# Summing the squares of eleven norms: three VectorE additions and one matmul, or eight matmuls on TensorE

## The chip, the core and the metric

The kernel runs on one core of a Trainium2 chip, as a single launch. The metric is the device time of that launch in microseconds, lower is better. The core has five engines that work side by side and wait for each other by semaphores: TensorE (PE, matrix products into PSUM), VectorE (DVE), ScalarE (ACT), GpSimd (POOL) and SyncE (SP, which issues most transfers). Each engine runs its own instructions strictly in the order in which the program lists them.

## The reference

Two blocks of a model, one after the other, on 1024 tokens of 1024 features, all in float32. The first: norm, input product, sliding-window attention and a chunked mLSTM, output product, cross attention over a memory of 256 tokens, and a feed-forward block with a short convolution. The second: norm with scale and shift from a condition vector, an RWKV-7 recurrence beside a banded attention, output product. What the change touches is the norm over the features:

```python
def rmsnorm(x, g):
    xf = x.astype(jnp.float32)
    y = xf * lax.rsqrt(jnp.mean(xf * xf, axis=-1, keepdims=True) + RMS_EPS)
    return (y * g.astype(jnp.float32)).astype(x.dtype)
```

It is taken of x before the mixing (`mix`), of x before the cross attention (`x`), of the memory (`mem`), before the feed-forward block (`ffn`), at the end of the first block (`fin`) and at the start of the second (`n2`). The kernel works in two halves of 512 tokens, so there are eleven norms: mix0, mix1, mem (256 tokens), x0, x1, ffn0, ffn1, fin0, n20, fin1, n21.

## The kernel before

Activations lie transposed: features on the 128 partitions, in 8 tiles `k`, and 512 tokens of one half along the free dimension. Every weight product keeps float32 accuracy by splitting both factors into a high part in the f32r type and a low part, with three matmuls of 512 columns for each `k` (function `mm`, lines L1171 to L1173, and `mmN`, L1191 to L1193). A tile of a product is 24 such matmuls; the down product has 66. Weights come in slabs of 512 KB in four slots. ScalarE copies a slab's high part (L2239), VectorE subtracts it to get the low part (L1636); both run up to three slabs ahead. A slab of `w_ada` (condition product, L1211) isn't split.

A norm is a list of steps, made by `rms` in class `Order`:

- `rms_sq`: eight squares on ScalarE (L2297), one for each `k`.
- `rms_add`: VectorE adds the squares of the eight tiles in pairs of tiles (L1731 twice, L1734, L1736) until one tile of 512 columns is left.
- `rms_sum`: TensorE multiplies that tile with a matrix of ones, in plain float32 (L1202), which sums over the partitions. VectorE makes the mean (L1741), ScalarE the root (L2302).
- `rms_rcp`: the reciprocal on VectorE (L1748).
- `rms_out`: for each `k` the output on VectorE (L1760) and, where a product follows, ScalarE's bias (L2308, only `n2`) and high part (L2312) and VectorE's low part (L1755).

The order of all work is laid out once, as a list of steps from which each engine takes its own. `rms` yields its steps in entries, and `weave` or `partly` puts one entry of a norm behind one entry of a product (a tile, or half or a quarter of one by the job's `cut`). For fin1 and n21 a planner, `flow`, chooses what comes next by estimated times from the function `work`; these steps stand behind the tiles of products lo0, k0, r0, v0 (these are the first products of the second block: their tiles end in a shift on VectorE, L1704 to L1713). After v0 come the head norm kk0 (squares L2420, sum L1390) and the `lora` products (L1454), whose constants SyncE may fetch (L2633) only when x has been written aside (L2621) and all outputs of n21 are done, because they use x's place. n20 stands at the end of product down1, the last of the first block.

Of the kernel before, what the change touches and what calls it, by code (L numbers as in the profile page):

```python
# [11 lines left out]
MUL, ADD, SUB, MAX, MIN = ALU.mult, ALU.add, ALU.subtract, ALU.max, ALU.min  # L12
# [30 lines left out]
class Signals:  # L43
# [4 lines left out]
    def __init__(self, take):  # L48
        self.take, self.sems, self.n, self.value, self.marks, self.strict = take, {}, {}, {}, {}, False
# [6 lines left out]
    def on(self, name, *event, by=1):  # L56
        self.n[name] = self.n.get(name, 0) + by
        assert self.value.setdefault((name, *event), self.n[name]) == self.n[name], (name, event)
        return self.sem(name), by
# [5 lines left out]
    def at(self, name, *event):  # L65
        assert not self.strict or (name, *event) in self.value, (name, event)
        return self.sem(name), self.value.get((name, *event), 1)
# [92 lines left out]
class Memory:  # L160
# [38 lines left out]
    def work(self, a, n):  # L199
        return self.f32(W0 + a, n)  # L200
# [9 lines left out]
    def cs(self, name, a=0, b=None):  # L210
        o, w = CST[name]
        return self.fixed["cst"][:, o + a:o + (w if b is None else b)]
# [4 lines left out]
    def bank(self, b):  # L217
        return self.PS[:, 512 * b:512 * b + 512]

    def parts(self, a, b, n=512):  # L220

        hi, lo = ([self.f32r(o + k * n, n) for k in range(8)] for o in (a, b))
        fhi, flo = ([self.f32(o + k * n, n) for k in range(8)] for o in (a, b))
        return hi, lo, fhi, flo, self.f32(a, 8 * n)

    def slot_raw(self, i, k, n):
        return v3(self.f32(G0 + 2048 * i, k * n), k)
# [11 lines left out]

    def first(self):  # L240
        work, f32, small = self.work, self.f32, self.small
        self.xh = [[f32(X0 + 4096 * h + 512 * k, 512) for k in range(8)] for h in range(2)]
        self.xs = [[self.XT[:, k, 512 * h:512 * h + 512] for k in range(8)] for h in range(2)]
# [88 lines left out]
class Norm:  # L332


    def __init__(self, src, ready, gain, parts, free=(), T=512, bias=None, to=None, extra=()):
        self.src, self.ready, self.gain, self.hi, self.lo, self.sq = src, ready, gain, parts[0], parts[1], parts[2]
        self.to, self.squares = to or parts[3], parts[4]
        self.split, self.free, self.T, self.bias, self.extra = to is None, list(free), T, bias, list(extra)


# [157 lines left out]
def work(step):  # L498

    name, *x = step  # L500
    if name == "mm":
        return [("pe", 3 * (x[5] - x[4]) * (0.227 if x[0].N == 512 else 0.12))]
    if name == "mmN":
        return [("pe", 0.681 * len(x[1]) * (x[4] - x[3]))]
    if name == "band_s":
        wide = min(5, x[1] + 1) / 5
        return [("pe", 1.1 * wide + 0.1), ("v", 1.7 * wide + 0.1)]
    if name == "band_p":
        return [("v", 0.2 + 1.5 * min(5, x[1] + 1) / 5)]
    if name == "band_x":  # L510
        return [("a", 0.2 + 0.85 * min(5, x[1] + 1) / 5)]
    if name == "band_t":
        return [("pe", 0.1 + 0.55 * min(5, x[1] + 1) / 5), ("a", 0.2 + 0.6 * min(5, x[1] + 1) / 5)]
    if name == "band_o":
        return [("pe", 0.1 + 1.1 * min(5, x[1] + 1) / 5)]
    if name == "rms_out":
        return [("v", 1.45), ("a", 1.3)] if x[0][:3] != "fin" else [("v", 0.7)]
    if name == "ev_shift":
        return [("a", 0.6), ("v", 1.45)] + ([("a", 0.65)] if x[0].name[0] == "g" else [])
    return {  # L520
# [15 lines left out]
    }.get(name, [])  # L536


class Order:
# [83 lines left out]
    def slab(self, w, k0, kn, c0, cn, parts=True):  # L623
        self.slabs.append((w, k0, kn, c0, cn, parts))
        return len(self.slabs) - 1
# [74 lines left out]
    def rms(self, tag):  # L700
        n = self.norms[tag]
        yield [("rms_sq", tag)]
        yield [("rms_add", tag, 0)]
        yield [("rms_add", tag, 1), ("rms_add", tag, 2)]
        b, free = self.banks.take()
        self.banks.give(b, ("rms.v", "mean", tag))
        yield [("rms_sum", tag, b, free)]
        b, free = self.pairs.take()
        steps = [("rms_rcp", tag, b, free)]
        for k in range(8):  # L710
            steps.append(("rms_out", tag, k, b))
            if k % 2 and k < 7:
                yield steps
                steps = []
        self.pairs.give(b, ("rms.v", "o", tag, 7))
        return steps
# [434 lines left out]
def tensor_program(pe, w, m, S, o):  # L1151

    on, at, bank, pair, cs = S.on, S.at, m.bank, m.pair, m.cs
# [42 lines left out]
    def rms_sum(tag, b, free):  # L1196
        n = o.norms[tag]
        w.wait_ge(*at("cst", 0))
        for e in S.each(free):
            w.wait_ge(*e)  # L1200
        w.wait_ge(*at("rms.v", "add", tag, 2))
        pe.matmul(bank(b)[:, 0:n.T], cs("ones"), n.sq[0], start=True, stop=True).then_inc(*on("rms.pe", "sum", tag))  # L1202

    def ada_mm(t, b, free, q):
        view = m.slot_raw(q % NSLOT, 8, 128)
# [396 lines left out]
    def seq_out(cp, b, free):  # L1602
# [3 lines left out]
        for j in range(4):  # L1606
# [4 lines left out]
              win_t=win_t, win_o=win_o, gates_f=gates_f, gates_t=gates_t, ml_e=ml_e, ml_q=ml_q, ml_s=ml_s, ml_k=ml_k,  # L1611
# [10 lines left out]
def vector_program(v, w, m, S, o):  # L1622

    on, at, bank, pair, small = S.on, S.at, m.bank, m.pair, m.small
# [97 lines left out]
        v.scalar_tensor_tensor(out=out, in0=bank(b), scalar=m.mod[:, 16 + t:17 + t], in1=out, op0=MUL,  # L1722
                               op1=ADD).then_inc(*on("gemm.v", "ev", j.name, t))

    def rms_add(tag, i):

        n = o.norms[tag]
        part = lambda k, c: n.squares[:, k * n.T:(k + c) * n.T]
        if i < 2:
            w.wait_ge(*at("rms.a", "sq", tag, 4 * i + 3))  # L1730
            v.tensor_tensor(part(4 * i, 2), part(4 * i, 2), part(4 * i + 2, 2), ADD).then_inc(*on("rms.v", "add", tag, i))  # L1731
        else:
            w.wait_ge(*at("rms.v", "add", tag, 1))
            v.tensor_tensor(part(0, 2), part(0, 2), part(4, 2), ADD).then_inc(*on("rms.v", "add4", tag))  # L1734
            w.wait_ge(*at("rms.v", "add4", tag))
            v.tensor_tensor(part(0, 1), part(0, 1), part(1, 1), ADD).then_inc(*on("rms.v", "add", tag, 2))  # L1736

    def rms_sum(tag, b, free):
        n = o.norms[tag]
        w.wait_ge(*at("rms.pe", "sum", tag))  # L1740
        v.tensor_scalar(n.sq[0], bank(b)[:, 0:n.T], 1.0 / 1024, 1e-6, MUL, ADD).then_inc(*on("rms.v", "mean", tag))  # L1741
# [460 lines left out]
    def fin_part(h, k, mark):  # L2202
# [2 lines left out]
        v.tensor_tensor(lo[k], m.src2[h][k], hi[k].bitcast(F32), SUB).then_inc(*on("fin.v", "lo", h, k))  # L2205

    do = dict(mark=lambda name: S.mark("v", name), slab=slab, ev_gate=ev_gate, ev_add=ev_add, ev_swish=ev_swish,
              ev_conv_m=ev_conv_m, ev_conv_f=ev_conv_f, ev_up=ev_up, ev_shift=ev_shift, ev_out=ev_out, rms_add=rms_add,
              rms_sum=rms_sum, rms_rcp=rms_rcp, rms_out=rms_out, ada_end=ada_end, win_s=win_s, win_t=win_t, gates_f=gates_f,
              gates_log=gates_log, gates_scan=gates_scan, gates_max=gates_max, gates_exp=gates_exp, gates_t=gates_t,  # L2210
              ml_e=ml_e, ml_q=ml_q, ml_s=ml_s, ml_c=ml_c, ml_o=ml_o, mix_parts=mix_parts, cross_s=cross_s,
              cross_t=cross_t, cross_o=cross_o, hs_fin=hs_fin, hs_t=hs_t, hs_o=hs_o, band_s=band_s,
# [487 lines left out]


PROGRAMS = (tensor_program, vector_program, scalar_program, gpsimd_program, sync_program)


# [133 lines left out]
```

## Time and profile before

| | us |
|---|---|
| median of 3 runs | 2795.58 (2793.31 to 2796.35) |
| the profiled execution, its own time | 2795.58 |
| its span in the profile | 2793.7 |
| TensorE matmuls busy | 2533.4 (91%) |
| VectorE busy | 1438.5 (51%) |
| ScalarE busy | 937.4 (34%) |

Busy is the time in which an engine's instructions ran; a matmul's end is modelled, so a busy TensorE is not TensorE at its peak. The chain is the work that ended last, followed back from the end at each step to what released it. A row of the timeline gives start, length, engine, line, operation, what is written from what, the count merged into the row, and in brackets the engine's idle time before it with its releaser. SR names tensors of the f32r type, SB plain ones in SBUF, PS PSUM. A plain float32 matmul leaves two records, an f32r matmul one. Some matmul records are missing.

### The profile page before, as it was taken

To read this page: it belongs to the slowest core of one execution; us is meant where nothing else is said; L and a number is where in the kernel's file an instruction comes from. 1 tells how busy PE (TensorE), PEld (TensorE's weight loads), DVE (VectorE), ACT (ScalarE), POOL (GpSimd) and SP (SyncE) were. 2 spreads that over 40 slices of the span, in tenths; PEclk is the share of its full clock that TensorE was granted. 3 is DMA by queue.
4 is the path that set the end of the run, shared out by engine and by line. 5 is a ranking of instruction groups with operands and counts; after the bars stand their busy time and mean duration, and the time that the engine had idled before them with its cause. 6 is when DMAs were issued, how large, how long until landed. Compare 5 with 4: busy or idle time off the path is not lost.

```text
span 2793.7 us, 40671 instructions
## 1 busy us (share of the span) xinstructions
PE 2533.4 (91%) x17602; PEld 2046.9 (73%) x17602; DVE 1438.5 (51%) x2444; ACT 937.4 (34%) x1572; POOL 82.2 (3%) x61
## 2 busy tenths in 40 slices
PE   4997878898988999999999998988999999589879
PEld 3785656787777878888888886756777777377757
DVE  5725665537332465544555545745344454666653
ACT  3323342224332333332333324354222232233341
POOL 0000000000000000000000000002000000200000
PEclk9998986889999999999999999978999999699989
DMA  4331110444411233333333333322312320211033
GB/s 133 90 100 47 55 35 16 128 144 118 131 46 53 68 92 97 98 95 98 96 97 98 97 96 109 113 73 76 110 58 62 99 62 24 102 38 38 10 117 117
DMA packets 370810, 233.00 MB, mean 83 GB/s; under 512 B 9796, under 2 KB 344772, under 8 KB 370504
## 3 DMA queue, kind: packets, MB, share of 16 engines
q1 hardware_dynamic: 367896, 224.83, 27.0%
q10 hardware_dynamic: 2736, 5.57, 0.5%
q8 instruction: 139, 2.28, 0.3%
q14 instruction: 39, 0.32, 0.0%
HBM read 211.50 MB, written 18.87 MB: 82 GB/s over the span
## 4 chain that ended last, share of the span: by engine, by line
PE 76%; DVE 14%; ACT 7%; issue 2%; DMA 1%; SPq 0%; DVEq 0%; ACTq 0%
PE PS L1171 17%; PE PS L1172 17%; PE PS L1173 17%; PE PS L1506 4%; PE PS L1157 3%; PE PS L1191 1%; DVE SR L1636 1%; PE PS L1193 1%; PE PS L1192 1%; ACT SR L2239 1%; PE PS L1211 1%; DVE SB L1676 1%; PE PS L1354 1%; PE PS L1424 1%; DVE SB L1760 1%
## 5 line engine op out<-in xcount | busy, mean ns | idle before, releaser
L1171 PE MATMUL PS<-SR 128*128 128x512 f32 (+2 forms) x2384 | 960.7, 403 | 50.2 <-DVE SR L1636 34.0
L1172 PE MATMUL PS<-SR 128*128 128x512 f32 (+2 forms) x2384 | 937.5, 393 | 0.0
L1173 PE MATMUL PS<-SR 128*128 128x512 f32 (+2 forms) x2384 | 935.9, 393 | 0.0
L1636 DVE TENSOR_TENSOR SR<-SB,SR 128x1024 fp32r<-128x1024 f32 (+2 forms) x328 | 395.3, 1209 | 455.6 <-ACT SR L2239 455.4
L1171 PEld LDWEIGHTS PS<-SR 128*128 128x128 f32 (+1 forms) x2384 | 457.1, 192 | 176.9 <-issue 39.0
L1173 PEld LDWEIGHTS PS<-SR 128*128 128x128 f32 (+1 forms) x2384 | 456.3, 191 | 97.2
L1172 PEld LDWEIGHTS PS<-SR 128*128 128x128 f32 (+1 forms) x2384 | 457.5, 192 | 90.9 <-issue 2.2
L2239 ACT ACTIVATE SR<-SB 128x1024 fp32r<-128x1024 f32 (+2 forms) x328 | 337.6, 1035 | 306.0 <-DMA SB<-in_w_down 110.2
L1157 PE MATMUL PS<-SB 128*128 128x128 f32 (+3 forms) x680 | 114.1, 308 | 73.1 <-DVE SB L1804 41.3
L1506 PEld LDWEIGHTS PS<-SB 64*64 64x64 f32 x4096 | 127.5, 135 | 37.6 <-issue 21.9
L1157 PEld LDWEIGHTS PS<-SB 128*128 128x128 f32 (+3 forms) x680 | 85.6, 157 | 92.9 <-DVE SB L1804 45.1
L1506 PE MATMUL PS<-SB 64*64 64x64 f32 x4096 | 140.0, 221 | 9.5 <-DVE SB L2120 5.7
L2246 ACT ACTIVATE SB<-PS 128x512 f32<-128x512 f32 (+2 forms) x86 | 44.8, 547 | 253.7 <-PE PS L1173 200.8
L1676 DVE SCALAR_TENSOR_TENSOR SB<-SB 128x512 f32<-128x512 f32 x136 | 102.3, 752 | 4.8
L1651 DVE TENSOR_TENSOR SB<-PS,SB 128x512 f32<-128x512 f32 x48 | 33.0, 690 | 132.3 <-PE PS L1173 128.5
L1191 PE MATMUL PS<-SR 128*128 128x512 f32 (+1 forms) x224 | 81.2, 362 | 5.9 <-DVE SR L1636 3.7
L1192 PE MATMUL PS<-SR 128*128 128x512 f32 (+1 forms) x224 | 80.0, 357 | 0.0
L1193 PE MATMUL PS<-SR 128*128 128x512 f32 (+1 forms) x224 | 80.0, 357 | 0.0
L2312 ACT ACTIVATE SR<-SB 128x512 fp32r<-128x512 f32 (+1 forms) x72 | 43.5, 608 | 90.8 <-DVE SB L1760 90.2
L2539 POOL TENSOR_TENSOR SB<-SB 128x512 f32<-128x512 f32 x8 | 16.5, 2062 | 1923.9 <-DVE SB L2030 1923.9
L2445 ACT ACTIVATE SB<-PS 128x640 f32<-128x640 f32 (+4 forms) x64 | 36.1, 569 | 96.0 <-PE PS L1157 95.7
L2268 ACT ACTIVATE SB<-PS 128x512 f32<-128x512 f32 x44 | 26.4, 601 | 124.1 <-PE PS L1173 124.1
(237 smaller groups left out, 2599.1 us busy)
## 6 DMA issues: line engine op xcount, KB each, us to landing
SB<-in_w_in SPq DMA_DIRECT2D x110, 512.0 KB, 4.0
SB<-in_w_up SPq DMA_DIRECT2D x88, 512.0 KB, 3.9
SB<-in_w_out SPq DMA_DIRECT2D x32, 512.0 KB, 3.8
SB<-in_w_down SPq DMA_DIRECT2D x32, 512.0 KB, 3.6
SB<-in_w_ada SPq DMA_DIRECT2D x24, 512.0 KB, 4.8
asides<-SB SPq DMA_DIRECT2D x40, 256.0 KB, 4.5
SB<-in_wkv SPq DMA_DIRECT2D x16, 512.0 KB, 3.9
SB<-in_wq SPq DMA_DIRECT2D x16, 512.0 KB, 3.7
```

The lines of the kernel that those rows point to most:

```text
L1157: return pe.transpose(out, in_, m.I[0:n, 0:n])
L1171: pe.matmul(out, whi[:, k - k0, :], hi[k], start=(k == 0), stop=False)
L1172: pe.matmul(out, whi[:, k - k0, :], lo[k], start=False, stop=False)
L1173: i = pe.matmul(out, wlo[:, k - k0, :], hi[k], start=False, stop=(k == j.K - 1))
L1191: pe.matmul(out, hi, whi[:, k - k0, :], start=(k == 0), stop=False)
L1192: pe.matmul(out, hi, wlo[:, k - k0, :], start=False, stop=False)
L1193: i = pe.matmul(out, lo, whi[:, k - k0, :], start=False, stop=(k == 7))
L1506: x = pe.matmul(bank(got[a][0])[ps, c:c + 64], lhs(a, q, j)[ps, :], rhs(a, q, j)[ps, :], start=True, stop=True)
L1636: v.tensor_tensor(m.f32r(a, kn * cn), m.f32(a, kn * cn), m.f32r(a + 1024, kn * cn).bitcast(F32), SUB).then_inc(*on("split.v", p))
L1676: v.scalar_tensor_tensor(out=out, in0=pad[:, i:i + 512], scalar=weight(i), in1=out, op0=MUL, op1=ADD).then_inc(*on("conv.v", "tap", j.name ...
L2239: a.activation(m.f32r(at_ + 1024, kn * cn), m.f32(at_, kn * cn), ACT.Copy).then_inc(*on("split.a", p))
L2246: a.activation(j.dst(t), src, j.func, scale=j.scale).then_inc(*on("gemm.a", "ev", j.name, t))
```

## The change

`rms_add` is gone: its two entries in `rms`, its step on VectorE and its estimate. TensorE's `rms_sum` now multiplies each of the eight tiles of squares with the ones and accumulates in PSUM, waiting for ScalarE's square `k` before matmul `k`. The planner's estimate of the sum goes from 0.9 to 6.9 us of TensorE. As `rms` has two entries fewer, what stands behind them comes two entries earlier.

```diff
-        "ev_add": [("v", 0.7)], "ev_out": [("v", 0.75)], "rms_sq": [("a", 5.0)], "rms_add": [("v", 1.25)],
-        "rms_sum": [("pe", 0.9), ("v", 0.7), ("a", 1.9)],
+        "ev_add": [("v", 0.7)], "ev_out": [("v", 0.75)], "rms_sq": [("a", 5.0)], "rms_sum": [("pe", 6.9), ("v", 0.7), ("a", 1.9)],
...
         yield [("rms_sq", tag)]
-        yield [("rms_add", tag, 0)]
-        yield [("rms_add", tag, 1), ("rms_add", tag, 2)]
         b, free = self.banks.take()
         self.banks.give(b, ("rms.v", "mean", tag))
         yield [("rms_sum", tag, b, free)]
...
-        w.wait_ge(*at("rms.v", "add", tag, 2))
-        pe.matmul(bank(b)[:, 0:n.T], cs("ones"), n.sq[0], start=True, stop=True).then_inc(*on("rms.pe", "sum", tag))
+        for k in range(8):
+            w.wait_ge(*at("rms.a", "sq", tag, k))
+            i = pe.matmul(bank(b)[:, 0:n.T], cs("ones"), n.sq[k], start=(k == 0), stop=(k == 7))
+        i.then_inc(*on("rms.pe", "sum", tag))
...
-    def rms_add(tag, i):
-
-        n = o.norms[tag]
-        part = lambda k, c: n.squares[:, k * n.T:(k + c) * n.T]
-        if i < 2:
-            w.wait_ge(*at("rms.a", "sq", tag, 4 * i + 3))
-            v.tensor_tensor(part(4 * i, 2), part(4 * i, 2), part(4 * i + 2, 2), ADD).then_inc(*on("rms.v", "add", tag, i))
-        else:
-            w.wait_ge(*at("rms.v", "add", tag, 1))
-            v.tensor_tensor(part(0, 2), part(0, 2), part(4, 2), ADD).then_inc(*on("rms.v", "add4", tag))
-            w.wait_ge(*at("rms.v", "add4", tag))
-            v.tensor_tensor(part(0, 1), part(0, 1), part(1, 1), ADD).then_inc(*on("rms.v", "add", tag, 2))
```

What moves with it is seen best at three places. The first is VectorE at the end of product down1, around the sum of n20. Before, behind the last tile's addition to x (L1651), stand the mean, the reciprocal and all eight outputs with their low parts:

```order
L1651 TENSOR_TENSOR SB<-PS,SB 128x512
L1741 TENSOR_SCALAR SB<-PS 128x512
L1748 RECIPROCAL PS<-SB 128x512
L1760 SCALAR_TENSOR_TENSOR SB<-SB,PS 128x512 x2
L1755 TENSOR_TENSOR SR<-SB,SR 128x512
L1760 SCALAR_TENSOR_TENSOR SB<-SB,PS 128x512
L1755 TENSOR_TENSOR SR<-SB,SR 128x512
```

After (lines above the sum are 1 smaller, those below it up to 14: L1650 is the addition to x, L1746 the output, L1741 the low part):

```order
L1635 TENSOR_TENSOR SR<-SB,SR 128x1024 x2
L1650 TENSOR_TENSOR SB<-PS,SB 128x512
L1746 SCALAR_TENSOR_TENSOR SB<-SB,PS 128x512
L1741 TENSOR_TENSOR SR<-SB,SR 128x512
L1746 SCALAR_TENSOR_TENSOR SB<-SB,PS 128x512
L1741 TENSOR_TENSOR SR<-SB,SR 128x512 x2
L1999 TENSOR_SCALAR SB<-SB 128x17
```

Six outputs, the reciprocal and the mean have moved ahead of that last tile; two outputs are left behind it.

The second place is VectorE behind the last tile of v0 (its shift is L1707 to L1713), with n21's outputs. Before:

```order
L1713 SCALAR_TENSOR_TENSOR SB<-SB 128x512
L1760 SCALAR_TENSOR_TENSOR SB<-SB,PS 128x512
L1755 TENSOR_TENSOR SR<-SB,SR 128x512
L1760 SCALAR_TENSOR_TENSOR SB<-SB,PS 128x512
L1755 TENSOR_TENSOR SR<-SB,SR 128x512
L1760 SCALAR_TENSOR_TENSOR SB<-SB,PS 128x512
```

After, from the last outputs of n21 to the shift of that last tile and the first step of the head norm (L1943):

```order
L1746 SCALAR_TENSOR_TENSOR SB<-SB,PS 128x512
L1741 TENSOR_TENSOR SR<-SB,SR 128x512 x2
L1703 MEMSET SB 128x1
L1706 COPY SB<-SB 128x1
L1710 TENSOR_SCALAR SB<-SB 128x512
L1712 SCALAR_TENSOR_TENSOR SB<-SB 128x512
L1635 TENSOR_TENSOR SR<-SB,SR 128x1024
L1943 TENSOR_SCALAR SB<-SB 128x32
```

Six outputs stood behind the last shift, and now none does.

The third is VectorE in the product kx, where x1 is woven in. Before, the additions stand between the splits of the weights:

```order
L1636 TENSOR_TENSOR SR<-SB,SR 128x1024 x4
L1731 TENSOR_TENSOR SB<-SB 128x1024
L1636 TENSOR_TENSOR SR<-SB,SR 128x1024
L1731 TENSOR_TENSOR SB<-SB 128x1024
L1734 TENSOR_TENSOR SB<-SB 128x1024
L1736 TENSOR_TENSOR SB<-SB 128x512
L1636 TENSOR_TENSOR SR<-SB,SR 128x1024
L1741 TENSOR_SCALAR SB<-PS 128x512
L1636 TENSOR_TENSOR SR<-SB,SR 128x1024
L1748 RECIPROCAL PS<-SB 128x512
```

After:

```order
L1635 TENSOR_TENSOR SR<-SB,SR 128x1024 x4
L1727 TENSOR_SCALAR SB<-PS 128x512
L1635 TENSOR_TENSOR SR<-SB,SR 128x1024
L1734 RECIPROCAL PS<-SB 128x512
L1746 SCALAR_TENSOR_TENSOR SB<-SB,PS 128x512 x2
```

The mean (L1727) and the reciprocal (L1734) stand two splits, that is two tiles of kx, earlier. From the head norm kk0 on, every engine has the order that it had.

## Rows read from the trace of the kernel before

**Rows 1.** The page's section 4: shares of the chain, by engine and line.
```profile
PE 76%; DVE 14%; ACT 7%; issue 2%; DMA 1%; SPq 0%; DVEq 0%; ACTq 0%
PE PS L1171 17%; PE PS L1172 17%; PE PS L1173 17%; PE PS L1506 4%; PE PS L1157 3%; PE PS L1191 1%; DVE SR L1636 1%; PE PS L1193 1%; PE PS L1192 1%; ACT SR L2239 1%; PE PS L1211 1%; DVE SB L1676 1%; PE PS L1354 1%; PE PS L1424 1%; DVE SB L1760 1%
```

**Rows 2.** Groups by line: busy, mean ns of one; idle before, its releaser.
```profile
L1202 PE MATMUL PS<-SB 128*128 128x512 f32 (+1 forms) x22 | 13.1, 679 | 26.4 <-DVE SB L1736 26.4
```

**Rows 3.** Windows: length; busy PE, PEld, DVE, ACT, POOL; granted clock; DMA; GB/s.
```profile
1640.00:1700.00 60.00, 60.00 (x264) 49.31 (x264) 25.01 (x26) 17.34 (x22) 0.00 (x0) 1.00 0.32 93
661.25:705.74 44.49, 35.53 (x218) 32.01 (x218) 30.39 (x33) 21.68 (x36) 0.00 (x0) 0.88 0.37 109
1731.00:1737.00 6.00, 6.00 (x14) 3.81 (x15) 5.65 (x9) 5.59 (x9) 0.00 (x0) 0.54 0.00 0
```

**Rows 4.** Timeline of VectorE and TensorE at the start, mix0.
```profile
17.64 1.22 DVE L1734 TENSOR_TENSOR SB<-SB 128x1024 f32<-128x1024 f32 x1
18.89 0.69 DVE L1736 TENSOR_TENSOR SB<-SB 128x512 f32<-128x512 f32 x1
...
19.73 2.04 PE L1202 MATMUL PS<-SB 128*128 128x512 f32 x2 [19.73 <-DVE SB L1736]
```

**Rows 5.** The chain in order of time (start, us): plain float32 matmuls of 512 and 256 columns.
```profile
62.99 0.86 PE PS L1202 x2
...
783.39 3.47 PE PS L1354 x16
```

**Rows 6.** Timeline of ScalarE: the squares of mix0.
```profile
12.08 4.26 ACT L2297 ACTIVATE SB<-SB 128x512 f32<-128x512 f32 x8 [8.32 <-DMA SB<-in_xT]
```

**Rows 7.** Timeline of TensorE: its waits near mix1, x0, x1 and ffn0.
```profile
135.23 0.50 PE L1191 MATMUL PS<-SR 128*128 128x512 f32 x1 [0.69 <-ACT SB L2258]
...
635.01 1.10 PE L1202 MATMUL PS<-SB 128*128 128x512 f32 x2 [1.74 <-DVE SB L1736]
...
661.25 0.58 PE L1171 MATMUL PS<-SR 128*128 128x256 f32 x1 [4.40 <-DVE SR L1636]
...
678.21 1.06 PE L1202 MATMUL PS<-SB 128*128 128x512 f32 x1 [2.35 <-DVE SB L1736]
...
705.74 0.50 PE L1191 MATMUL PS<-SR 128*128 128x512 f32 x1 [1.77 <-DVE SR L1636]
...
1004.81 0.50 PE L1171 MATMUL PS<-SR 128*128 128x512 f32 x1 [1.29 <-DVE SR L1755]
```

**Rows 8.** Timeline of VectorE: the mean and the last low part of x1.
```profile
680.17 0.69 DVE L1741 TENSOR_SCALAR SB<-PS 128x512 f32<-128x512 f32 x1 [0.96 <-PE PS L1202]
...
703.52 0.69 DVE L1755 TENSOR_TENSOR SR<-SB,SR 128x512 fp32r<-128x512 f32 x1
```

**Rows 9.** Timeline of TensorE: n20's sum, then tiles lo0 and k0.
```profile
1721.88 0.39 PE L1173 MATMUL PS<-SR 128*128 128x512 f32 x1
1722.11 0.59 PE L1202 MATMUL PS<-SB 128*128 128x512 f32 x1
1730.98 0.77 PE L1171 MATMUL PS<-SR 128*128 128x512 f32 x1 [7.86 <-DVE SR L1755]
...
1740.59 0.50 PE L1171 MATMUL PS<-SR 128*128 128x512 f32 x1 [0.32 <-DVE SR L1755]
```

**Rows 10.** Timeline of TensorE: the sums of fin1 and n21, head norm, lora.
```profile
1754.14 0.70 PE L1202 MATMUL PS<-SB 128*128 128x512 f32 x1 [1.71 <-DVE SB L1736]
...
1795.63 0.67 PE L1202 MATMUL PS<-SB 128*128 128x512 f32 x1 [0.87 <-DVE SB L1736]
...
1824.61 1.65 PE L1390 MATMUL PS<-SB 128*128 128x2 f32 x7 [12.88 <-ACT SB L2420]
...
1829.91 2.08 PE L1454 MATMUL PS<-SB 64*128 64x512 f32 x4
```

**Rows 11.** Timeline of SyncE: the fetch of the constants.
```profile
1824.74 0.34 SPq L2633 DMA_DIRECT2D SB<-in_lora  x1
```

**Rows 12.** DMA issues from 1800 to 1850 us: KB, us to landing.
```profile
spill<-SB SPq DMA_DIRECT2D x1, 2048.0 KB, 9.3
```

More of the change, by code:

```diff
@@ L223, in parts @@
         fhi, flo = ([self.f32(o + k * n, n) for k in range(8)] for o in (a, b))
-        return hi, lo, fhi, flo, self.f32(a, 8 * n)
+        return hi, lo, fhi, flo
     def slot_raw(self, i, k, n):
@@ L336, in __init__ @@
         self.src, self.ready, self.gain, self.hi, self.lo, self.sq = src, ready, gain, parts[0], parts[1], parts[2]
-        self.to, self.squares = to or parts[3], parts[4]
+        self.to = to or parts[3]
         self.split, self.free, self.T, self.bias, self.extra = to is None, list(free), T, bias, list(extra)
@@ L2207, in vector_program @@
     do = dict(mark=lambda name: S.mark("v", name), slab=slab, ev_gate=ev_gate, ev_add=ev_add, ev_swish=ev_swish,
-              ev_conv_m=ev_conv_m, ev_conv_f=ev_conv_f, ev_up=ev_up, ev_shift=ev_shift, ev_out=ev_out, rms_add=rms_add,
-              rms_sum=rms_sum, rms_rcp=rms_rcp, rms_out=rms_out, ada_end=ada_end, win_s=win_s, win_t=win_t, gates_f=gates_f,
+              ev_conv_m=ev_conv_m, ev_conv_f=ev_conv_f, ev_up=ev_up, ev_shift=ev_shift, ev_out=ev_out, rms_sum=rms_sum,
+              rms_rcp=rms_rcp, rms_out=rms_out, ada_end=ada_end, win_s=win_s, win_t=win_t, gates_f=gates_f,
               gates_log=gates_log, gates_scan=gates_scan, gates_max=gates_max, gates_exp=gates_exp, gates_t=gates_t,
```

## The prediction

> **What bounds the kernel now.** I read the page's chain first: TensorE holds 76% of it, 51% of the span in the three f32r lines of the weight products [rows 1]. So a microsecond put on TensorE is paid unless it falls into one of its idle times. Next I read the lines of the norm: 11 sums, 22 records (each f32 matmul leaves two), 13.1 us in all, and 26.4 us of TensorE's idle time ended by L1736, the last VectorE addition [rows 2]. 19.73 of these are the start of the program [rows 4]; the other 6.7 are four waits of 0.9 to 2.4 us [rows 7, 8, 10], so the additions are a small bottleneck at most. Last I followed each of the 11 norms in the timelines. They differ: fin0 sits in a stretch where TensorE never stops (busy for 60.00 of 60 us [rows 3]), and ffn1 in one just like it; others have an idle time behind or before the sum, and two end a stage with TensorE waiting for the norm itself.
>
> **What the change costs per norm.** It takes away four VectorE additions (three of 1.22 us, one of 0.69 [rows 4]) and adds 7 matmuls of the f32 form. Eight such matmuls of 256 columns take 3.47 us back to back (16 records), and one of 512 columns takes 0.86 us of the chain [rows 5]; so 0.434 us per 256 columns, 0.867 per 512, and 7 more cost 6.07 us, or 3.04 for the memory norm with its 256 columns. All eight read the same weights "ones", but the loads are hidden beside the matmuls in the row I use, so nothing is gained or lost there. The Trainium skill, "TensorE: Matmul & The Clock Gate", section Back-to-back issue gap, says that a stream of weight load and matmul pairs runs at about 131 ns for each 512 columns, and in "FP8 and Floating Point Precision", section TensorE Precision Notes, that true f32 takes four passes. By the two a sum would cost 0.52 us, not 0.87, an estimate from those pages. The trace disagrees on the first: f32r matmuls of 512 columns, each with its own weights, start 0.23 us apart [rows 9], and four of these are 0.91.
>
> A second effect is as large: two fewer entries in the norm's list. Each entry is paired with one tile of the product it is woven into, so the sum, the reciprocal and the eight outputs all come two entries earlier on every engine. The sum now waits for ScalarE's squares directly. Eight squares take 4.26 us [rows 6], 0.53 each, faster than TensorE sums them, and one tile of 5.4 us stands between the order to square and the sum; so I expect no wait where that tile is a full one.
>
> **Norm by norm.**
> - mix0: nothing hides it. Squares run 12.08 to 16.34 us; the additions end at 19.6 and the sum at 21.8 [rows 4, 6]. Now the sum starts at about 12.7. The lone matmul there takes 2.04 us, against 0.86 later: TensorE stood before it and runs at 1.2 GHz. After the idle time at n20 the granted clock is 0.54 over the first 6 us, so some 5.3 us at half rate and then the full one [rows 3, 9]. A sum matmul at half rate is 2 x 0.867 = 1.73. If it is the same here, 3.1 matmuls are slow and 4.9 fast, and the sum ends at 12.7 + 5.3 + 4.2 = 22.2: +0.5. If all stay slow, 12.7 + 8 x 1.73 = 26.5: +4.8. I take +0.5, as the nearest row has the rate rise.
> - mix1: +6.07. Its last outputs no longer stand ahead of the next product's convolutions on VectorE, so the one wait there, 0.69 us [rows 7], goes: +5.4.
> - mem: 3.04, nothing back. If its squares were not done, up to 2.6 us of wait (eight squares of 256 columns at half of 0.53, and some) would come on top; I take none.
> - x0: 6.07, +0.4 for the squares, which queue behind mem's last two outputs. The wait for the addition goes (1.74), and so does the 4.40 us before 661.25 [rows 7]: there the splits of the next weights stand behind x0's last outputs on VectorE, which now finish tiles earlier. Net +0.3.
> - x1: 6.07, but this stage is bound by VectorE (TensorE is busy 35.5 of 44.5 us, VectorE 30.4 with its waits for ScalarE between [rows 3]). mean, sqrt, reciprocal, outputs and three splits are one chain. Before, mean ended at 680.86 and the outputs at 704.2 [rows 8]. TensorE comes 3.4 us late into the stage, the sum, two tiles of about 3 us earlier and 6.9 long, ends at 679.2, the mean at 680.0, so the chain ends 0.9 earlier, but two slabs that were already multiplied are left. The third slab of vx0 starts at 710.8, against 705.74 [rows 7]: +5.1 in all, 1.7 from this norm.
> - ffn0: 6.07 less the wait of 1.3 us for late outputs [rows 7]: +4.8.
> - ffn1, fin0: +6.07 each; there is no idle time to win back [rows 3].
> - n20: before, its sum, reciprocal and outputs all stand behind the last tile of down1. From that sum (1722.11) to the next stage's second tile (1740.59) go 18.48 us, with 7.86 idle and then a granted clock of 0.54 [rows 3, 9]. One sum and one tile need 0.9 + 5.44. Now only outputs 6 and 7 are left behind down1, and the last is needed 4.8 us into the next tile, some 0.1 us late. So 12.0 come back: -5.9.
> - fin1: 6.07 - 1.71 [rows 10] = +4.4.
> - n21: 6.07 - 0.87 [rows 10], and the end of the stage: TensorE's first matmul after the last v0 tile starts at 1824.61, after 12.88 us of idle, because ScalarE finishes six of n21's outputs before it squares for the next head norm, and the constants are fetched only once they are done, at 1824.74 [rows 10, 11]. Some records of the tile are missing: by 24 x 0.227 us it ends at 1812.9. The first lora matmul starts at 1829.91 [rows 10], 17.0 later. Now two outputs are left, done before the tile ends. What then stands between the tile and lora is an eviction and what stands there today after the first square: 1829.91 - 1823.9 = 6.1 and 1.0 before it, 7.1 us in all; the spill of x, issued as the tile starts and landing 9.3 us later [rows 12], so some 4 us after its end, and the fetch behind it (about 3 us) allow the same. 9.9 come back: -4.7.
>
> **Sum.** Gross: 9 x 6.07 + 3.04 + 0.5 = 58.2 us. Back: 0.7 (mix1) + 5.7 (x0) + 4.4 (x1) + 1.3 (ffn0) + 12.0 (n20) + 1.7 (fin1) + 10.8 (n21) = 36.6. Net +21.6. The profiled execution took 2795.58 us with a span of 2793.7, and it is the median of the three. So 2817.2 us. Everything after this stage has its old order on every engine, so I carry the difference to the end unchanged.
>
> **Rivals.**
> - Tail stays: n21's outputs don't end in time, because VectorE, now with a reciprocal and an output pair inside one tile, falls behind. Then 9.9 are not given back: 2827. For it: the pairs wait for ScalarE's bias and copy each time. Against: the planner leaves a tile between most pairs.
> - New waits: the sum stands so near its squares that TensorE, in order, stops. Worst where the squares are themselves late: x0, fin1, n21, up to 4.3 us each: about +12, 2829.
> - Nothing comes back: each stage merely ends later by its sums and the old waits reappear in front of something else: 2854. 2795.6 + 58.2. Against it: 7.86 and 12.88 us of idle whose releaser moves [rows 9, 10].
> - More comes back than I count, mostly mix1, whose convolution chain on VectorE starts 3.4 us later and not 6, and x1: 2807.
> - Not slower: the sums are cheap. 36.6 us stand against 66.5 new matmuls of 512 columns' worth, so 0.55 us for one instead of 0.87 breaks even, and below it the kernel is faster. It is a mechanism of this one instruction: with the same weights in succession its passes could run closer than with changing ones. The matmuls of [rows 5] change weights each time and don't exclude it; against it, records of full width start no closer than 0.23 us [rows 9]. At 0.52 it would end at 2794 (2795.6 + 34.6 + 0.5 - 36.6). 0.52 is also what the two pages of the Trainium skill named above give.
>
> **How the numbers follow.** Forecast 55% (2811 to 2824 by itself), tail stays 12%, new waits 11%, nothing back 6%, more back 10%, cheap sums 6%. The range 2805 to 2836 leaves out the cheap sums, the dearest case and a little of each side. A change under 0.2% (5.6 us) can't be told from none: faster 3%, same 5%, slower 92%.
>
> **What would show it.** L1200 (the sum) with 176 records, about 0.43 us apart for 512 columns; no idle time after n20's sum; the gap before the first matmul of the head sum after v0 down from 12.9 to about 2 us; the wait before kx gone; the sums at the start first at half rate. The forecast is wrong if the sums' records stand closer, if TensorE's idle time ended by ScalarE's squares passes 3 us in all, or if the end of v0 keeps its long gap.

## The result, and the profile after

The changed kernel takes 2821.4 us (2819.8 to 2827.2), 1.010 times the time before (95% interval 1.0081 to 1.0120). This is the median of three executions; with a fourth, slow one of 8742.9 us at a granted clock of 0.416, the median is 2824.3. In a second session it took 2820.9 us beside 2791.1, a ratio of 1.0105 (1.0092 to 1.0119). The forecast was 2817.2 us with a range of 2805 to 2836: the side and the range held, and the middle was 4 us too low. The difference is the stricter measure, as the kernel before varies too: +21.6 us were forecast and +29.8 measured (25.7 to 33.2, second session), so 8 us were missing.

The profiled execution of the changed kernel took 2809.28 us with a span of 2807.4. It is faster than all its timed ones, so I took a second profile, of an execution of 2821.55 us, and read both. The page of the first: span, chain (section 4), and the group of the sum, with what answers to [rows 1, 2].

```profile
span 2807.4 us, 40934 instructions
...
PE 81%; DVE 11%; ACT 5%; DMA 2%; issue 1%; SPq 0%; DVEq 0%; ACTq 0%
...
L1200 PE MATMUL PS<-SB 128*128 128x512 f32 (+1 forms) x176 | 75.6, 583 | 13.7 <-ACT SB L2283 13.7
```

TensorE's share of the chain rose from 76 to 81%, and the sum (L1200) is now 3% of the span, with 176 records. Of its 13.7 us of idle time 13.16 are the start of the program; so all the waits of TensorE for squares come to half a microsecond here, and to 1.2 in the second profile (0.95 of it before mem's sum). Next the timeline of TensorE in the first profile, with the sums of mix0, mem, x0, x1, ffn0, fin0, fin1 and n21, the first weights after x0, and the head norm after v0 [rows 4, 7, 10].

```profile
13.16 8.70 PE L1200 MATMUL PS<-SB 128*128 128x512 f32 x16 [13.16 <-ACT SB L2283]
...
599.54 3.62 PE L1200 MATMUL PS<-SB 128*128 128x256 f32 x16
...
620.93 7.11 PE L1200 MATMUL PS<-SB 128*128 128x512 f32 x16 [0.51 <-ACT SB L2283]
...
653.21 0.79 PE L1168 MATMUL PS<-SR 128*128 128x512 f32 x1 [2.88 <-DVE SR L1635]
...
675.88 7.03 PE L1200 MATMUL PS<-SB 128*128 128x512 f32 x16
...
969.98 7.03 PE L1200 MATMUL PS<-SB 128*128 128x512 f32 x16
...
1644.73 7.03 PE L1200 MATMUL PS<-SB 128*128 128x512 f32 x16
...
1755.62 7.03 PE L1200 MATMUL PS<-SB 128*128 128x512 f32 x16
...
1788.37 7.03 PE L1200 MATMUL PS<-SB 128*128 128x512 f32 x16
...
1837.07 1.05 PE L1389 MATMUL PS<-SB 128*128 128x2 f32 x8 [2.20 <-ACT SB L2406]
```

A sum of eight matmuls takes 7.03 us at full clock to its last modelled end, where the single one of the chain took 0.86 [rows 5], and 3.62 us for the 256 columns of mem. The wait of 12.88 us before the head sum (the sum of the head norm kk0) is 2.20. One wait is new: 2.88 us before 653.21, where the splits of the next weights (L1635) come late on VectorE. The queue of SyncE after v0, in the first profile, against [rows 11]: the constants are fetched at 1840.05, 3 us after the head sum begins, where they waited for n21's outputs before.

```profile
1829.87 0.58 SPq L2607 DMA_DIRECT2D spill<-SB  x1
1840.05 0.34 SPq L2619 DMA_DIRECT2D SB<-in_lora  x1
```

To see where the time went I followed the same evictions (the instructions that take a finished tile of a product out of PSUM) through both traces. The table gives what each stage adds against the first profile of the kernel before. The times of that profile stand at its head; "same code" are executions of other kernels of this study, and of the one before, whose code in the stage is that of before. The boundary at 600 is the last tile ahead of mem's sum, the one at 740 lies behind x1's norm.

```
us, stage of before     0-25  25-150  150-600  600-740  740-955  955-1024  1024-1332  1332-1851  1851-end
forecast                +0.5    +5.4        0     +5.0        0      +4.8       +6.1       -0.1         0
after, 1st profile      +0.1    +4.3     -4.2     +9.6     -6.3      +3.7       +6.0       +0.1      +0.3
after, 2nd profile      +1.3    +4.3     -3.6    +13.7     -0.1      +3.7       +6.0       -0.2      +0.8
same code, lowest       -0.9     0.0     -8.8     -0.6     -6.2       0.0        0.0       -0.4      -0.2
same code, highest      +1.0     0.0      0.0     +4.3      0.0      +1.5        0.0        0.0      +6.4
same code, mean         +0.2     0.0     -6.3     +0.9     -2.4      +0.2        0.0       -0.1      +3.5
executions of it          11       9        9        7        9         8          9          4         9
```

Where TensorE hardly stops the stages repeat to a few hundredths (25 to 150, 1024 to 1332), and 1332 to 1851 does to 0.4 us. Four others (150 to 600, 600 to 740, 740 to 955, and from 1851 on) move by 5 to 9 us with no change in their code, so there a single pair of profiles says little, and only a mean or a timed run does.

### The profile page after: what moved, and what is told of

Read it like the earlier page. It is cut to its first block, busy times and chain, and to the rows that moved or that the text cites. A ratio compares the mean times of both kernels' runs of the same rounds, so it can differ in the third digit from the quotient of the medians.

```text
span 2807.4 us, 40934 instructions
## 1 busy us (share of the span) xinstructions
PE 2580.0 (92%) x17756; PEld 2066.4 (74%) x17756; DVE 1394.0 (50%) x2400; ACT 936.2 (33%) x1572; POOL 82.2 (3%) x61
## 4 chain that ended last, share of the span: by engine, by line
PE 81%; DVE 11%; ACT 5%; DMA 2%; issue 1%; SPq 0%; DVEq 0%; ACTq 0%
PE PS L1168 18%; PE PS L1169 18%; PE PS L1170 18%; PE PS L1505 4%; PE PS L1154 3%; PE PS L1200 3%; PE PS L1188 2%; PE PS L1190 2%; PE PS L1189 2%; PE PS L1210 1%; PE PS L1423 1%; PE PS L1443 1%; PE PS L1353 1%; ACT SB L2314 1%; PE PS L1389 1%
## 5 line engine op out<-in xcount | busy, mean ns | idle before, releaser
L1635 DVE TENSOR_TENSOR SR<-SB,SR 128x1024 fp32r<-128x1024 f32 (+2 forms) x328 | 395.3, 1208 | 463.7 <-ACT SR L2225 463.4
L1650 DVE TENSOR_TENSOR SB<-PS,SB 128x512 f32<-128x512 f32 x48 | 33.0, 689 | 131.7 <-PE PS L1170 127.7
L1200 PE MATMUL PS<-SB 128*128 128x512 f32 (+1 forms) x176 | 75.6, 583 | 13.7 <-ACT SB L2283 13.7
```

Of the source, the lines that this page charges most:

```text
L1200: i = pe.matmul(bank(b)[:, 0:n.T], cs("ones"), n.sq[k], start=(k == 0), stop=(k == 7))
L1635: v.tensor_tensor(m.f32r(a, kn * cn), m.f32(a, kn * cn), m.f32r(a + 1024, kn * cn).bitcast(F32), SUB).then_inc(*on("split.v", p))
```

## The experiments

Each was timed in five rounds beside the kernel before.

**Eight matmuls, but the entries of the list kept.** Two empty entries stand where the additions were.

```diff
         yield [("rms_sq", tag)]
+        yield []
+        yield []
```

> The changed kernel, but with two empty entries in each norm's list where the additions stood: eight sum matmuls, no additions, and the sum, the reciprocal and the outputs at their old places. My theory (the matmuls cost 0.87 us for each 512 columns and are paid in full; the earlier places give back some 37 us): this one gets nothing back but the waits for the additions (1.7 at x0, 0.9 at n20 and n21, 1.7 at fin1), so 2795 + 58 - 5 = 2848, 2838 to 2855, and the 7.9 and 12.9 us of idle time at the end of down1 and of v0 stay. Rival (the places matter little; what came back did so because the additions are gone from VectorE): about 2822, like the changed kernel.

It took 2836.2 us, ratio 1.0155 (1.0140 to 1.0169): between the two theories, and 2 us below my range. Its timeline of TensorE, at n20 and before the head sum:

```profile
1770.62 0.77 PE L1170 MATMUL PS<-SR 128*128 128x512 f32 x1 [7.86 <-DVE SR L1743]
...
1866.30 1.02 PE L1391 MATMUL PS<-SB 128*128 128x2 f32 x4 [6.02 <-ACT SB L2408]
```

n20 keeps its 7.86 us to the hundredth, so that gain is the place's. But the wait before the head sum is 6.02 us, not 12.9. fin1 and n21 stand in the part that the planner places by its prices, where an empty entry ends at once; two of n21's outputs were left behind v0 instead of six. From 1332 to 1851 it adds 14.7 us, the changed kernel 0.1 and -0.2: the places are worth 15 us there, 1.7 at mix1 (6.0 against 4.3) and 2.3 at ffn0 (6.0 against 3.7). By the medians they are worth 15 us in all. I had put nearly all of the 36.6 us that come back down to the places. In truth 58.2 - 29.8 = 28 come back, if the 58.2 of the forecast stand as the full price of the matmuls, and about half of that isn't the places': it goes with the additions that are gone and with the planner's prices, which no run here tells apart.

**The additions kept, the places taken.** In one kernel the additions stand in the entry of the squares, in the other in the entry of the sum.

```diff
-        yield [("rms_sq", tag)]
-        yield [("rms_add", tag, 0)]
-        yield [("rms_add", tag, 1), ("rms_add", tag, 2)]
+        yield [("rms_sq", tag), ("rms_add", tag, 0), ("rms_add", tag, 1), ("rms_add", tag, 2)]
```

> The kernel before, with its additions and its single sum matmul, but the three additions stand in the same entry as the squares, so that the sum, the reciprocal and the outputs come two entries earlier, as in the changed kernel. My theory (earlier places give back 37 us, and only the matmuls cost): 2795 - 37 plus some us where VectorE stands before an addition for squares that aren't done (4.3 us of squares, 11 norms, partly hidden): 2765, 2758 to 2778. Rival (VectorE, now stopped before the splits of the next tile, starves TensorE in each norm by about 3 us): 2790 or more.

```diff
         yield [("rms_sq", tag)]
-        yield [("rms_add", tag, 0)]
-        yield [("rms_add", tag, 1), ("rms_add", tag, 2)]
-        yield [("rms_sum", tag, b, free)]
+        yield [("rms_add", tag, 0), ("rms_add", tag, 1), ("rms_add", tag, 2), ("rms_sum", tag, b, free)]
```

> As the one with the early additions, but the three additions stand in the sum's entry, one tile after the squares, so VectorE never waits for squares and TensorE may wait for the additions (4.35 us on VectorE). My theory: the same 37 us back, less up to 1 to 2 us per norm where TensorE waits for the last addition: 2768, 2758 to 2782. Rival (TensorE waits for additions in full, 4.4 us in each of nine norms, which eats the gain): 2795.

They took 2808.5 us (1.0059; 1.0045 to 1.0072) and 2853.8 us (1.0223; 1.0209 to 1.0237), 43 and 86 us above what my theory said. The rivals had the mechanism: 2790 or more for the first, and 2795 for the second, which was 59 us too low as well. TensorE in the first (mem, x0, x1, fin1) and then in the second (fin0, n20, fin1, n21):

```profile
603.00 0.77 PE L1200 MATMUL PS<-SB 128*128 128x256 f32 x1 [6.00 <-DVE SB L1734]
632.91 2.05 PE L1200 MATMUL PS<-SB 128*128 128x512 f32 x2 [7.12 <-DVE SB L1734]
...
689.50 1.19 PE L1200 MATMUL PS<-SB 128*128 128x512 f32 x1 [5.02 <-DVE SB L1734]
...
1748.85 1.19 PE L1200 MATMUL PS<-SB 128*128 128x512 f32 x1 [5.81 <-DVE SB L1734]
```

```profile
1667.77 1.19 PE L1200 MATMUL PS<-SB 128*128 128x512 f32 x1 [5.13 <-DVE SB L1734]
...
1721.54 1.19 PE L1200 MATMUL PS<-SB 128*128 128x512 f32 x1 [5.13 <-DVE SB L1734]
...
1786.63 1.19 PE L1200 MATMUL PS<-SB 128*128 128x512 f32 x1 [10.28 <-DVE SB L1734]
...
1839.97 2.05 PE L1200 MATMUL PS<-SB 128*128 128x512 f32 x2 [9.84 <-DVE SB L1734]
```

In the early places one tile stands between order and sum. One of 24 matmuls takes 5.4 us, which covers the squares (4.26 us, [rows 6]) but not squares and additions (three of 1.22 and one of 0.69 us, [rows 4]) one after the other. At x0 the squares also begin late, at 625.27, behind mem's last two outputs, and the additions end at 632.8. A tile of down1 has 66 matmuls, some 15 us, and covers both: before the sums of fin0 and n20 the first kernel doesn't wait. The sum of eight matmuls needs no additions and starts with the first square. So the early places were not free in every norm with the additions kept: the change pays TensorE's time for a chain that is shorter by the additions, and the shorter chain is what makes the early places free.

**The changed kernel again**, unaltered.

> The changed kernel once more, unaltered, for the spread of its time: one profiled execution took 2809.3 us, three timed ones 2819.8 to 2827.2. Theory (the difference lies in where the granted clock falls in the stages with short idle times; in the profiled execution cross attention had two half-rate stretches where the kernel before had four): the times again spread over 2808 to 2828, longer ones with the lower mean granted clock. Rival (the profiled execution was one of a kind for another reason, such as the start of the program): all within 3 us of 2821, no matter what the clock is.

2820.9 us (2819.2 to 2821.8, four executions at clocks of 0.939 to 0.941). No execution was as fast as the first profile. The four lie within 3 us, as the rival said, and not over 2808 to 2828; the stages, though, differ as the theory has it (-6.3 and -0.1 us from 740 to 955). The kernel before shows the same more plainly. **The kernel before again**, unaltered:

> The kernel before once more, unaltered, for a second profile of it and as a null: ratio 1.000 within 0.002. Theory (gaps in the stages with short idle times differ between executions of one program): the idle time of 4.40 us before kx's first matmul comes out at 1 to 2 us, those of 7.86 us at n20 and 12.88 us before the head sum come out the same to 0.1 us. Rival (all idle times are fixed by the order): 4.40 again.

Ratio 1.0002 (0.9988 to 1.0017), with executions from 2784.6 us (granted clock 0.943) to 2799.4 (0.936), 0.5% apart. Its TensorE, at the first weights of kx, at n20, and before the head sum:

```profile
654.48 0.39 PE L1171 MATMUL PS<-SR 128*128 128x256 f32 x1 [0.91 <-DVE SR L1636]
...
1717.69 0.76 PE L1171 MATMUL PS<-SR 128*128 128x512 f32 x1 [7.86 <-DVE SR L1755]
...
1811.28 1.02 PE L1390 MATMUL PS<-SB 128*128 128x2 f32 x4 [12.89 <-ACT SB L2420]
```

The 7.86 and 12.88 us are there again, and the 4.40 us of [rows 7] are 0.91. In four other kernels, whose code here is the same, I read 0.89, 1.04, 1.48 and 4.23. It was no fixed wait, and I had counted it as one that comes back. The windows of 730 to 960 us, of the first profile of the kernel before and then of this one (length; busy PE, PEld, DVE, ACT, POOL; granted clock; DMA; GB/s):

```profile
730.00:960.00 230.00, 213.25 (x1055) 183.09 (x1056) 74.58 (x110) 68.81 (x133) 0.00 (x0) 0.94 0.20 60
```

```profile
730.00:960.00 230.00, 213.25 (x1091) 182.65 (x1090) 76.49 (x111) 70.81 (x133) 0.00 (x0) 0.99 0.20 60
```

One program, the same busy time but 36 more records of matmuls in it, a clock of 0.94 and of 0.99, and 6.1 us between them by the evictions. The Trainium skill, "TensorE: Matmul & The Clock Gate", section on the HAM clock gate (Part 1), says that the number of slow matmuls at the start of a kernel varies from run to run with the phase of the gate. The traces show such a variation in the middle of a kernel (0.94 and 0.99); that the phase is its reason, no run here shows.

**Parts of the change.** The next kernels are the one before with lists of norms: those in DIRECT have the changed kernel's list and its eight matmuls, those in EARLY have their additions in the entry of the squares, all others are as before.

```diff
+        if tag in DIRECT:
+            yield [("rms_sq", tag)]
+        elif tag in EARLY:
+            yield [("rms_sq", tag), ("rms_add", tag, 0), ("rms_add", tag, 1), ("rms_add", tag, 2)]
+        else:
+            ...
```

**mem and x0 alone**, and **x0 alone**:

```diff
+DIRECT = ('mem', 'x0')
+EARLY = ()
```

> The kernel before, with eight sum matmuls, no additions and the two entries fewer only for the norms mem and x0. It asks for the price of this stage alone, which the prediction put at 3.0 + 0.3 us. In two profiled executions of the changed kernel the stage cost 6.8 and 11.2 us, and with old places 7.1. Theory (the matmuls' 9.1 us are paid, 1.7 us of waiting for the addition comes back, and of the 4.4 us before the next weights only about 2 do, since a wait of 2.5 to 2.9 us for splits stands behind x0's outputs; the rest of the 11.2 is the clock's phase): +5.5, 2793 to 2801 beside 2791. Rival (the prediction's own figure): +3.3 or less. Second rival (the stage truly costs 11): +11.

```diff
+DIRECT = ('x0',)
+EARLY = ()
```

> The kernel before, with eight sum matmuls, no additions and the two entries fewer only for the norm x0. With mem too it was 9.2 us slower (5.9 to 12.8). The prediction put x0 at +0.3 and mem at +3.0. Theory now (6.07 for the matmuls, less the wait of 1.7 for the addition; the 4.4 us before the next weights were an accident of the one profile, 1.0 to 1.5 us in others, and a wait of 2.5 for splits takes their place): +5, 2791 to 2799. Rival (the prediction's own figure): +0.3. Second rival (nothing at all comes back): +6 or more, with mem then 3.

The first took 2799.7 us, 1.0033 (1.0021 to 1.0046), that is +9.2 us (5.9 to 12.8) where the forecast had 3.3 and my new theory 5.5; the second rival's 11 lies in the interval. In its profile mem's sum waits 2.52 us for its squares, a wait that the forecast named and put at none. The same profile, of its second slowest execution (2806.24 us), adds 16.9 us from 600 to 740 and takes 8.8 back ahead of it, which shows how little a single profile says here. The second took 2795.7 us, 1.0019 (1.0005 to 1.0034), that is +5.3 (1.4 to 9.5) where the forecast had 0.3 and the new theory 5; that nothing at all comes back (6) isn't excluded. Its stage from 600 to 740 adds 7.3 us, or 6.4 above the mean of the same code. TensorE in the one with x0 alone:

```profile
642.72 0.79 PE L1182 MATMUL PS<-SR 128*128 128x512 f32 x1 [2.11 <-DVE SR L1653]
```

This is the wait that was 2.88 us in the changed kernel and 2.47 in its second profile. VectorE ahead of it, in that second profile:

```profile
640.96 3.35 DVE L1734 RECIPROCAL PS<-SB 128x512 f32<-128x512 f32 x1
...
655.95 2.35 DVE L1635 TENSOR_TENSOR SR<-SB,SR 128x1024 fp32r<-128x1024 f32 x2
```

Between the two stand x0's eight outputs with their low parts, and only then come the splits. So x0's earlier outputs stand in front of the splits of a tile of out1 (the output product of the second half, into which mem and x0 are woven), the last but one, as before they stood in front of kx's.

**n20 alone**:

```diff
+DIRECT = ()
+EARLY = ('n20',)
```

> The kernel before, with all its additions and single sums, but n20's three additions stand in the entry of its squares, so its sum, reciprocal and outputs come two entries earlier. Nothing else is changed. Theory (the 12.0 us at the end of down1 are the place's alone and don't need the matmuls): -12, 2777 to 2782 beside 2791, and the wait of 7.86 us is gone. Rival (without the additions' absence VectorE is too late and the idle time only moves in front of the sum): within 5 us of before.

2794.6 us, 1.0015 (1.0004 to 1.0026): +4 us and not -12. The rival was right: the 7.86 us are gone, and a longer wait stands before the sum.

```profile
1687.95 2.05 PE L1214 MATMUL PS<-SB 128*128 128x512 f32 x2 [9.73 <-DVE SB L1753]
```

fin0 was still at its old place. Since one and a half entries go with a tile of down1, n20's sum now stood behind its squares with no tile between. It waits 9.73 us for them and the additions; VectorE just ahead of it, with its own waits for the squares:

```profile
1682.52 1.23 DVE L1748 TENSOR_TENSOR SB<-SB 128x1024 f32<-128x1024 f32 x1 [2.25 <-ACT SB L2314]
1684.60 1.23 DVE L1748 TENSOR_TENSOR SB<-SB 128x1024 f32<-128x1024 f32 x1 [0.85 <-ACT SB L2314]
1685.86 1.23 DVE L1751 TENSOR_TENSOR SB<-SB 128x1024 f32<-128x1024 f32 x1
1687.12 0.69 DVE L1753 TENSOR_TENSOR SB<-SB 128x512 f32<-128x512 f32 x1
```

**The same with fin1 and n21 of the changed kernel**:

```diff
+DIRECT = ('fin1', 'n21')
+EARLY = ('n20',)
```

> As the one before it (n20 earlier, with additions), and fin1 and n21 as in the changed kernel: eight sum matmuls, no additions, the planner's places. Against that one it asks for the price of fin1 and n21, which the prediction put at +4.4 - 4.7. Theory: within 2 us of it, so -12 beside before: 2775 to 2783; the wait before the first head sum after v0 falls from 12.88 to about 2.2 us. Rival (the saving of 10 us belongs to the full change only): 10 us slower than the one before it.

2794.2 us, 1.0021 (1.0010 to 1.0032). The 2775 to 2783 us were missed by n20's 9.73 us, as in the kernel before it. The theory held for the difference: from 1332 to 1851 it adds 3.5 us where n20 alone adds 5.8, so fin1 and n21 cost -2.3, and the wait before the head sum is 2.20 us (row 1822.14 of its timeline). **A mixed version**, with fin1's additions in one entry of their own behind that of the squares:

```diff
+DIRECT = ('n21',)
+EARLY = ('n20',)
...
+        elif tag == "fin1":
+            yield [("rms_sq", tag)]
+            yield [("rms_add", tag, 0), ("rms_add", tag, 1), ("rms_add", tag, 2)]
```

> A try at a better version: the kernel before, with n20 two entries earlier with its additions, fin1 one entry earlier with its additions, and n21 with eight sum matmuls and no additions. Theory: -12 for n20, +6.1 - 0.9 for n21's sum and -6.9 of the wait before the first head sum (6.0 us left, as in the kernel with eight matmuls at old places), fin1 within 2: -13.7, 2774 to 2782. Rival (fin1's additions, a tile earlier, stop TensorE as they did where they stood early, 5.8 us): -8.

2797.9 us, 1.0031 (1.0016 to 1.0045). It waits 9.73 us at n20 as well, 2.10 at fin1's sum and 6.93 before the head sum. fin1 and the head sum came out near what was expected (within 2, and 6.0); n20 spoilt it.

**fin0 and n20 together**, and with them **ffn0, fin1 and n21**:

```diff
+DIRECT = ()
+EARLY = ('fin0', 'n20')
```

> The kernel before with additions and single sums everywhere, the three additions in the entry of the squares for both fin0 and n20, so that n20's sum has a tile between it and its squares. Theory (the 12 us at the end of down1 come with the place once fin0 is done early too, additions or not; where only n20 was moved its sum stood right behind its squares and waited 9.7 us): the idle time of 7.86 us goes, less some 2 us of new waits: -10, 2777 to 2784 beside 2790. Rival (only eight matmuls, which start while squares are still made, can stand so near them): a wait of 5 us or more before a sum, and within 4 us of before.

```diff
+DIRECT = ('fin1', 'n21')
+EARLY = ('ffn0', 'fin0', 'n20')
```

> A try at a better version: as the one before it, ffn0's additions in the entry of its squares too, and fin1 and n21 with eight sum matmuls and no additions at the planner's places. Theory: -10 for the pair, -2 for ffn0 (14.1 to 11.2 where all additions stood early), -1.3 for fin1 and n21 (as between the shifts of the two kernels that differed in them): -13, 2773 to 2782. Rival (the parts don't add up, since the clock's phase takes it back): as the one before it or slower.

The pair took 2782.9 us, 0.9961 (0.9946 to 0.9976), and the second 2776.7 us, 0.9941 (0.9920 to 0.9962): 14 us less than before, and faster than both kernels. Both lie in the ranges expected. From 1332 to 1851 they add -10.0 and -11.1 us, from 955 to 1024 the second adds -2.3. TensorE in the second, in down1, at the first tile behind it, and before the head sum:

```profile
1665.64 0.50 PE L1182 MATMUL PS<-SR 128*128 128x512 f32 x1 [0.96 <-DVE SR L1653]
...
1697.95 0.50 PE L1182 MATMUL PS<-SR 128*128 128x512 f32 x1 [1.19 <-DVE SR L1653]
...
1804.39 0.83 PE L1407 MATMUL PS<-SB 128*128 128x2 f32 x6 [2.20 <-ACT SB L2437]
```

With a tile of down1 between n20's squares and its sum the additions are free, and in the second kernel the idle times of 7.86 and 12.88 us are both gone (in the pair the 12.89 stays), at the price of waits of 0.96 and 1.19 us for splits. Eight matmuls pay, by 1 to 2 us, in fin1 and n21 together (-11.1 against -10.0 here, 3.5 against 5.8 above), where the waits that they shorten come to more than they cost; no other norm showed that. The early places with the additions kept don't do it there: the kernel with all additions early adds -5.2 us from 1332 to 1851, with waits of 5.81 and 2.60 us before the sums of fin1 and n21 and of 6.93 before the head sum.

## Why the prediction was right, and where not

- **Price of a matmul: right.** Forecast 0.867 us for 512 columns. The stage from 1024 to 1332, which holds ffn1 alone, adds 6.00 us for seven in both profiles; 6.07 were forecast. The rival of cheap sums is out: it needed under 0.55, and these are 0.86.
- **End of down1 and of v0: right.** fin0, n20, fin1 and n21 together were forecast at -0.1 and came to +0.1 and -0.2. The wait of 12.88 us fell to 2.20 (about 2 forecast); behind n20's sum there is no idle time, with one of 1.19 us at the splits of the next product. The rival "tail stays" is out. The split of the credit was wrong in thought, not in number: I gave n20's 12 us to the two entries fewer alone, and the runs show that they come back only where the chain of squares and additions fits: n20 alone gives +5.8 us in this part, with fin0 -10.0. I also took one entry for one tile, and in down1 one and a half go with a tile.
- **New waits: right to be small.** TensorE waits 0.5 and 1.2 us for squares, under the 3 that would have made the forecast wrong.
- **mix0: right.** Forecast +0.5, measured +0.1 and +1.3. The sum starts at 13.16 and takes 8.70 us, 1.7 more than the 7.03 elsewhere (2.7 more in the second profile), so its first matmuls are slow and the others not. The 5.3 us at half rate were read a little short: a granted clock of 0.54 over 6 us gives 5.5, which moves the sum by 0.1 us.
- **mix1 and ffn0: a little too dear.** +5.4 and +4.8 forecast, +4.3 and +3.7 measured, in every execution alike. Each gave back 1.1 us more than the one wait that I subtracted.
- **x0: this term failed.** "The wait for the addition goes (1.74), and so does the 4.40 us before 661.25 ... Net +0.3." Alone it costs +5.3 us (1.4 to 9.5). The 4.40 us were no fixed wait (0.91 in the second profile), so they could not be counted as coming back, and a wait of 2.1 to 2.9 us came up for the splits of out1's last tile but one. With mem and x1 the stage costs 9 and 13 us above the mean of the same code, where 5.0 were forecast. x0 accounts for 5.0 of the missing 5.7 us; mem with x0 costs 3.9 more than x0 alone, with 3.0 forecast, but the intervals are too wide to tell these. x1 was not run alone.
- **150 to 600 us: not in the forecast.** Nothing is changed there, and the changed kernel is 2.4 us slower than the mean of nine executions of the same code (-4.2 and -3.6 beside -6.3). From 1851 on it is 2.9 us faster than the mean (+0.3 and +0.8 beside +3.5). Both stages have short idle times and a clock that falls and rises; whether the later start decides how often it falls, or two profiles are too few, stays open.

The parts above the means come to 0.5 + 4.3 + 2.4 + 10.7 - 0.8 + 3.5 + 6.0 + 0.0 - 2.9 = 23.7 us. The timed runs of the second session say 29.8 by the medians (25.7 to 33.2 by the interval). The rest, some 6 us, was not traced. The stages that repeat leave no room for it, so it should lie in those whose clock varies: the timed executions of the changed kernel ran at 0.938 to 0.941, its first profile at 0.945. That the middle of the forecast came within 4 us of the time is in part luck: what the stage of x0 cost too much was in part made up by mix1 and ffn0 (2.2 us less than forecast together), and the kernel before was itself 4 us faster in the second session than in the execution that I started from.

## What to carry to other kernels

Moving a reduction from VectorE to a saturated TensorE costs its full matmul time; what it buys is a shorter chain, and that is worth it only at the norms whose result TensorE itself waits for. Ask of each place whether the chain of square, addition and sum fits into the tiles that stand between them: if it does, as at n20, the same early place is free with the additions kept. Take a second profile of the same kernel before counting on an idle time to come back: here 7.86 and 12.88 us repeated to a hundredth of a microsecond, and 4.40 did not.

## What was not expected of the hardware

The granted clock of a stretch with short idle times is not a property of the program. From 730 to 960 us the same kernel had 0.94 and 0.99, and the part from 740 to 955 took 6.1 us less at the second. From 150 to 600 nine executions of one code lay 8.8 us apart. Where TensorE never stops, as from 1024 to 1332, the lengths of all nine executions of one code agree to 0.01 us.
